# A hybrid streaming encoder step: value parts of forgetting attention whole in a turn's last gap, value transposes ahead of it

## The reference, cut to what matters

```
for l in range(DEPTH):                       # 2 layers, 1024 prompt tokens and 64 sample tokens
    h = rms_norm(xp, ln_mix[l])
    qa, ka, va, la, qb, kb, vb = project_heads(h, w_in[l], b_f[l])
    ...
    # group A, forgetting attention: 8 heads x 64, causal, decay from the cumulative log-forget bias
    s = einsum('bqhd,bkhd->bhqk', q, k) * FOX_SCALE
    p = softmax(where(causal, s + decay, NEG))
    o = einsum('bhqk,bkhd->bqhd', p, v)
    ...
    xp = xp + o @ w_out[l]                   # with group B, sliding-window attention
    xp = xp + cross_attend(rms_norm(xp, ln_mem[l]), w_mq[l], mk, mv, w_mo[l])   # 4 heads x 128, 256 memory tokens
    f, cst = conv_ffn(rms_norm(xp, ln_ffn[l]), ...)
    xp = xp + f
```

## Time and profile before

| what | value |
|---|---|
| median of three timed runs | 3396.98 us (3394.63 to 3397.58) |
| profiled execution, its own time | 3382.89 us |
| its span in the trace | 3381.1 us |
| mean granted clock of TensorE | 0.992 |
| TensorE busy (matmul) | 3227.5 us |
| DVE, ACT, POOL busy | 1897.2, 846.9, 1213.6 us |

### The profile page before, as it was taken

How to read it: one execution, slowest core, us unless ns; L and a number is a source line. 1 busy time by engine, 2 the same in 40 slices (tenths; PEclk the granted TensorE clock), 3 DMA queues, 4 the chain that set the end, 5 groups by cost and what they waited for, 6 DMA issues and landing times.

```text
span 3381.1 us, 50293 instructions
## 1 busy us (share of the span) xinstructions
PE 3227.5 (95%) x20496; PEld 3110.0 (92%) x20496; DVE 1897.2 (56%) x3536; ACT 846.9 (25%) x1960; POOL 1213.6 (36%) x976
## 2 busy tenths in 40 slices
PE   7999998999999999999999999989999999999997
PEld 7888898888899999999988988978889999999997
DVE  6555567676744444444665655577666444444446
ACT  4432323543310000000233333155433000000002
POOL 5213222532434333333442222333424333334331
PEclk9999999999999999999999999999999999999998
DMA  4111222211111111111121112221101111111111
GB/s 160 51 52 45 64 58 69 67 43 33 35 44 47 44 44 44 41 45 46 42 78 58 50 40 58 76 73 48 54 26 41 44 44 46 43 44 47 44 44 65
DMA packets 86021, 177.57 MB, mean 53 GB/s; under 512 B 10544, under 2 KB 13872, under 8 KB 85392
## 3 DMA queue, kind: packets, MB, share of 16 engines
q1 hardware_dynamic: 71968, 132.90, 13.6%
q10 hardware_dynamic: 13824, 41.46, 4.2%
HBM read 150.36 MB, written 16.29 MB: 49 GB/s over the span
## 4 chain that ended last, share of the span: by engine, by line
PE 80%; DVE 11%; ACT 5%; issue 2%; POOL 1%; DMA 0%; ACTq 0%; SPq 0%; DVEq 0%; POOLq 0%
PE PS L614 80%; DVE ACC L1631 2%; ACT PR L1259 1%; DVE HL L1623 1%; DVE PR L1712 1%; DVE XT L1755 1%; ACT PW L1259 1%; DVE PW L1712 1%; ACT PTH L1111 1%; DVE XT L1585 1%; DVE PTL L1557 1%; POOL WL L594 1%; POOL WH L592 0%; DVE DG L1670 0%; ACT G0H L1111 0%
## 5 line engine op out<-in xcount | busy, mean ns | idle before, releaser
L592 POOL TENSOR_TENSOR WH<-RAW,zero 128x512 fp32r<-128x512 f32 x484 | 549.4, 1135 | 2082.0 <-PE PS L614 2067.4
L614 PE MATMUL PS<-HH,WH 128*128 128x384 f32 (+1 forms) x3312 | 863.8, 333 | 41.1 <-DVE HL L1623 16.2
L614 PE MATMUL PS<-HH,WL 128*128 128x384 f32 (+1 forms) x3312 | 848.6, 328 | 0.0
L614 PE MATMUL PS<-HL,WH 128*128 128x384 f32 (+1 forms) x3312 | 848.1, 328 | 0.0
L594 POOL TENSOR_TENSOR WL<-RAW,WH 128x512 fp32r<-128x512 f32 x484 | 669.3, 1383 | 37.9
L614 PEld LDWEIGHTS PS<-HH,WH 128*128 128x128 f32 x3312 | 586.7, 188 | 59.3 <-issue 18.4
L614 PEld LDWEIGHTS PS<-HL,WH 128*128 128x128 f32 x3312 | 589.7, 188 | 0.0
L614 PEld LDWEIGHTS PS<-HH,WL 128*128 128x128 f32 x3312 | 589.0, 188 | 0.0
L1755 DVE TENSOR_TENSOR XT<-PS,XT 128x320 f32<-128x320 f32 x464 | 314.3, 719 | 264.1 <-PE PS L614 263.9
L614 PE MATMUL PS<-G0H,WH 128*128 128x384 f32 (+1 forms) x960 | 274.5, 338 | 25.7 <-DVE XT L1585 17.1
L1111 ACT ACTIVATE PTH<-PS 128x512 fp32r<-128x512 f32 (+4 forms) x320 | 165.9, 521 | 520.1 <-PE PS L614 518.7
(11 more groups left out here) (255 smaller groups left out, 4709.1 us busy)
## 6 DMA issues: line engine op xcount, KB each, us to landing
RAW<-in_slabs SPq DMA_DIRECT2D x484, 256.0 KB, 2.6
XR<-decays ACTq DMA_DIRECT2D x16, 512.0 KB, 5.8
XT<-in_xT SPq DMA_DIRECT2D x8, 544.0 KB, 8.5
out_fk<-T ACTq DMA_DIRECT2D x8, 544.0 KB, 2.7
XR<-decays ACTq DMA_DIRECT2D x16, 272.0 KB, 7.0
out_fv<-T ACTq DMA_DIRECT2D x8, 544.0 KB, 2.9
out_y<-YT ACTq DMA_DIRECT2D x8, 544.0 KB, 3.1
RX<-ST ACTq DMA_DIRECT2D x24, 136.0 KB, 2.5
```

Of the source, the lines that this page charges most:

```text
L592: pool.tensor_tensor(WH[:, s, :], RAW[:, s, :], zero[:, 0:1].to_broadcast([128, HALF]), ALU.add).then_inc(w_hi, 1)
L614: ins = pe.matmul(*a, **k)
```

## The change

Three tables and the places that call for value transposes are edited. In fox_fill the parts of the next pair are dealt two to a turn, in gaps 0 and 1 of the turns 12, 13 and 14, and each value part stands whole in gap 2 of the turns -1, 0 and 1. The value transposes of pairs 1 to 3 are cut in two: the first two groups run in turn 1 behind the scores and ahead of gap 2, the other two in turn 2 behind the scores. V_GROUPS goes from 3, 2, 2, 2 tiles to 3, 3, 2, 1. In mem_fill the first part of head 2's queries stands in the gaps 0 and 1 of turn -1, ahead of the first scores, and the other two in gap 2 of the turns 0 and 1. ACT and DVE call their halves in the same turns.

```diff
@@ fox_fill
-            fill = {n - 1: spread(k[:2], (0, 1, 2)), n: spread(k[2:] + q[2:] + q[:1], (0, 1, 2)), n + 1: spread(q[1:2], (0, 1, 2))}
+            fill = {n - 1: spread(k[:2], (0, 1)), n: spread(k[2:] + q[2:], (0, 1)), n + 1: spread(q[:2], (0, 1))}
             if pair:
                 v = tile_parts(("v", pair), "T32")
-                fill |= {-1: spread(v[:1], (2,)), 0: spread(v[1:2], (0, 1, 2)), 1: spread(v[2:], (0, 1, 2))}
+                fill |= {c - 1: spread(v[c:c + 1], (2,)) for c in range(len(CH))}
@@ mem_fill
-            fill = {c - 1: spread(third[c:c + 1], (0, 1, 2)) for c in range(len(CH))}
+            fill = {c - 1: spread(third[c:c + 1], (2,) if c else (0, 1)) for c in range(len(CH))}
...
-        V_GROUPS = [[0, 1, 2], [3, 4], [5, 6], [7, 8]]
+        V_GROUPS = [[0, 1, 2], [3, 4, 5], [6, 7], [8]]
@@ TensorE
-            def value_hook(pe, filled):
-                value_tiles(pe, T32, V_GROUPS, own_values, filled)
-
+            def value_hook(pe, groups):
+
+
+                value_tiles(pe, T32, groups, own_values, (third_free, place.at("third", 1)))
                 held_groups[:] = [place.at("group", 2)] * len(held_groups)
@@ attention
                         scores(pe, steps[s + 1])
+                    if s in ahead_of_gap:
+                        ahead_of_gap[s]()
                     parts(pe, fill, s, 2)
@@ layer
-                        hooks = {2: lambda: value_hook(pe, (third_free, place.at("third", 1)))}
-                    attention(pe, fox_steps(pair), fox_fill(pair), hooks)
+                        between = {1: lambda: value_hook(pe, V_GROUPS[:2]), 2: lambda: value_hook(pe, V_GROUPS[2:])}
+                    attention(pe, fox_steps(pair), fox_fill(pair), {}, between)
@@ ACT, and DVE likewise
-                    hooks = {2: own_values} if pair else {0: own_values}
+                    hooks = {0: lambda: own_values(V_GROUPS)}
+                    if pair:
+                        hooks = {1: lambda: own_values(V_GROUPS[:2]), 2: lambda: own_values(V_GROUPS[2:])}
```

More of the change, by code:

```diff
@@ L992, in values, with attention @@
                     signal(w_used)
-            def attention(pe, steps, fill, hooks):
+            def attention(pe, steps, fill, hooks, ahead_of_gap={}):
                 rings = [0]
@@ L1026, in layer @@
                 project(pe, ("q", 0), HH, HL, CH)
-                own = project(pe, ("v", 0), HH, HL, CH)
+                project(pe, ("v", 0), HH, HL, CH)
                 pe.wait_ge(const_ok, 5)
@@ L1030, in layer @@
                     if pair == 0:
-                        hooks = {0: lambda: value_hook(pe, own)}
+                        between = {0: lambda: value_hook(pe, V_GROUPS)}
                         if l == 0:
-                            hooks[1] = lambda: mem_stat(pe)
+                            between[1] = lambda: mem_stat(pe)
                     else:
-                        hooks = {2: lambda: value_hook(pe, (third_free, place.at("third", 1)))}
-                    attention(pe, fox_steps(pair), fox_fill(pair), hooks)
+                        between = {1: lambda: value_hook(pe, V_GROUPS[:2]), 2: lambda: value_hook(pe, V_GROUPS[2:])}
+                    attention(pe, fox_steps(pair), fox_fill(pair), {}, between)
                     if pair == 1:
@@ L1355, in layer, with own_values @@
                 for pair in range(PAIRS):
-                    def own_values():
-                        value_groups(act, V_GROUPS, own_rows)
+                    def own_values(groups):
+                        value_groups(act, groups, own_rows)
                     def value_store():
@@ L1848, in own_rows, with own_values @@
                     return 128 if tile < NB else DEC
-                def own_values():
-                    value_groups(dve, V_GROUPS, own_rows)
+                def own_values(groups):
+                    value_groups(dve, groups, own_rows)
                 keys()
```

## The result

| | before | after |
|---|---|---|
| median (lowest to highest), us | 3395.81 (3384.43 to 3397.58), 4 runs | 3356.87 (3356.51 to 3363.65), 4 runs |
| profiled execution, us | 3382.89 | 3357.14 |
| its span, us, and mean granted clock | 3381.1, 0.992 | 3355.3, 0.991 |

The changed kernel is faster: the ratio is 0.9896, interval 0.9865 to 0.9926. I had said 3372 with a range of 3363 to 3384; 3356.87 lies under the range. The two profiled executions differ by 25.8 us, which is near the sum that I had worked out (24.9). The two medians differ by 38.9. So one question of this study was where the other 13 us are.

The account below looks back on a forecast made before the run. TensorE, busy 95% of the span, was taken as the bound, so only its waits could be won. Terms of 9.7, 0.6, 5.9, 0.8, 3.4, 0.7, 3.2 and 0.6 sum to 24.9; 3396.98 - 25 = 3372 us, range 3363 to 3384.

Parts of the forecast that it names:

- Cover: Between value parts and between query parts: other TensorE work hides the evictions, removing 12 waits of 0.81 and 8 of 0.74.
- The split: Value transposes of pairs 1 to 3 in two turns: 3.28 against 3.84 us, 0.56 saved a pair, 3.4 in all.
- The 1.72: Turn 2 of pairs 1 to 3: step 1's transposes come 1.72 us after the scores, a sum of chain pieces.
- The worry about what is queued behind it: Turn 1's new wait and step 0's transposes behind part 2: chains under 2.5 us, beneath 3.5 us of part 2.
- Pair 0: First value transposes of each layer: the wait for V shrinks by 0.35 us a layer, 0.7 in all.
- Memory: Head 2's memory queries: 4 waits of 0.81 go, 3.2 us, plus 0.6 for restarts; the 0.77 diagonal wait stays.
- the carry to the median: Last step: the profiled execution's 14 us below the timed median is kept, so 25 comes off 3396.98, giving 3372.
- A: Whole kernel: the saving comes as summed, 25 us, range 3366 to 3378; chance 0.74.
- B: Value groups and evictions: waits move to new places, only 15 us remain, 3382; chance 0.10.
- C: Stretches at half clock after pair 0's wait: up to 5 and 3 us more come back, 3364; chance 0.08.
- D: Window attention's start: the freed time is waited for later, nothing measurable, 3393 to 3399; chance 0.04.
- E: Value groups 0 and 1 late on ACT shift turn 2: slower by 0.2%, 3404; chance 0.04.

Follow-up runs that it names:

- e3: The kernel before with only the value parts put whole in the last gap, value transposes left in turn 2; 3377.63 us, ratio 0.9966.
- e2: The kernel before with only the next pair's parts dealt two by two; 3383.44 us, ratio 0.9995.
- e4: The kernel before with only the parts of head 2's memory queries moved; 3384.18 us, ratio 0.9998.
- e5: The changed kernel run again without edit, beside the kernel before; 3358.82 us, ratio 0.9903.
- e10: The changed kernel run once more without edit, on another chip beside the kernel before; 3363.27 us, ratio 0.9932.
- e6: The changed kernel with all value transposes of pairs 1 to 3 back in turn 2, groups 3, 2, 2, 2; 3369.65 us, ratio 0.9938 to before.
- e7: The changed kernel with pair 0's value transposes cut in two, over turns 0 and 1; 3358.47 us, ratio 0.9902 to the kernel before.
- e1: The kernel before, unchanged, run again beside itself; 3385.63 us, ratio 0.9999.

## Why the prediction was right, and where it failed

**The working was right, and the sum nearly.** 24.9 us were forecast, 25.8 lie between the two profiles, 27.1 at equal clock. The rows can be added without the fit: 2.65 for each of six pairs, 0.89 for each of eight pair ends and 1.44 for memory in each layer (both below, layer 1 taken as layer 0) are 25.9. So the last 1.2 us of the 27.1 stand in no row that I read.

| part | forecast | at equal clock |
|---|---|---|
| value parts whole (12 waits of 0.81, restarts) | 9.7 + 1.2 for the parts alone | 12.0 (e3) |
| next pair's parts two by two | 5.9 + 0.8 | 8.1 (e2) |
| memory queries | 3.2 + 0.6 | 3.3 (e4) |
| value transposes split, groups, pair 0 | 3.4 + 0.7 - 0.6 for one start more | 4.7 (e5, e10 less e6) |

The parts add to 28.1, the whole is 27.1. The difference is within the fit's error, so no hindrance between them is seen.

*Cover.* All 16 + 8 waits went, as said. The terms for them are a little small (12.0 and 8.1 for 10.9 and 6.7), about 0.1 us for each wait, which is at or just above what the fit can tell. At pair 0's end the trace gives 0.89 us for the 0.84 forecast, or 7.1 for all eight: from query part 2 to pair 1's scores 143.03 to 158.00 after the change, 143.43 to 159.29 before.

*The split.* I had called this the least sure term. It follows from 176.99 to 184.83, 7.84 us, where before took 9.95: 2.11 less, to set against the 1.56 us that six tiles cost in turn 1, which turned out as 1.31 (172.09 to 173.40). That is 0.80 a pair and 4.8 in all, beside the 4.7 of e6 and the 3.4 forecast: this is the term that was sized too small, since twelve transposes cost less in turn 1 than the 0.122 us each that I had taken from before. The 1.72 that I had built up from four rows was measured as 1.73. The worry about what is queued behind it did not come true: step 0's transposes wait 0.60 for PTL, as before.

*Pair 0.* 0.7 us forecast, and in the waits it is nothing: 2.09 and 2.36 became 1.85 and 2.70. In layer 0 my reason held, two matmuls more lie ahead of the same release. In layer 1 the chain itself began late. DVE's rows there, after the change:

```profile
1728.68 1.28 DVE L1717 CUSTOM_DVE_ANT_0 PR<-PS,XR,big 128x1024 f32<-128x1024 f32 x1 [0.81 <-DMA XR<-decays]
...
1733.48 1.02 DVE L1562 TENSOR_TENSOR V<-PS,V 128x384 fp32r<-128x384 f32 x2 [3.08 <-ACT V L1114]
```

The same maxima waited 0.25 us for that load before. Here time freed earlier was waited for again, 0.56 us of it.

*Memory.* From the start of the first part to step 1's transposes it is 16.20 us (745.70 to 761.90) after, 17.64 before (758.85 to 776.49): 1.44 less in layer 0 for the 1.9 forecast. No wait is left behind the shortest cover, six matmuls that take 0.82 us from start to the next part (755.17 to 755.99). I had said that the wait of 0.77 for the diagonal stays as it is; it grew, and is 0.97 in e4, e5 and e10 too:

```profile
761.90 1.16 PE L614 MATMUL PS<-DG,PW 128*128 128x128 f32 x8 [0.98 <-DVE DG L1675]
```

**The step that failed** is the last one, the carry to the median: "The difference is carried to the median: 3396.98 - 25". I took the 14 us between the profiled execution and the median of three for something that belongs to every timed run. It belongs to the clock of single executions. The kernel before runs at any level from 0.984 to 0.993, its times from 3381.6 to 3406.8 go with it, and of 69 later runs only a quarter came out at 3395 or more; its median over them is 3387.70. The changed kernel's first four runs stood at 0.990 to 0.992. So of the 38.9 us between the medians shown, some 27 are the change, and some 12 are that three of the four runs of before took far longer than its usual time, while those of after were near their shortest. The clocks of the first three runs of before are not listed; that they stood near 0.987, as runs of 3396.9 do, is inferred from the table and not seen. Had the sum been taken from the profiled execution, 3382.89 - 25, it would have given 3358, and 16 runs of the changed kernel have a median of 3358.8. Nor was the measured time outside the range by luck alone: 3358.8 lies under it too. The range was drawn from what the change might do, and held no room for the spread of one kernel's executions.

**The rivals.** A was right in its mechanism, and its own range (3366 to 3378) suffers from the same step. B, the waits move, was wrong for this change, though right for e7. C spoke of the clock, but of two stretches in the changed kernel. Those did change somewhat: 77.5 to 87.4 went from 0.52 to 0.66, and e10's execution has 0.83 there. In all, windows of 5 us give seven stretches at half clock before and eight after. I had called a change of that number a sign of being wrong, but it is none: e1, with no change at all, has thirteen. The mean clock over all runs is 0.9895 before and 0.9902 after, 1.8 us by the slope. What C should have asked is at which clock the *before* was timed. D and E did not occur.

## What to carry to other kernels

Here every wait of TensorE behind the eviction of its own bank went entirely once other work of at least that length stood between (0.81 us from start to start, printed as 0.65). Sum such waits from the distances of starts, not from what is printed, and add what a saved restart costs, here 0.1. If the profiled execution and the median of a few runs differ by more than the runs should, find out by the granted clock which of them is unusual before adding anything: a forecast made from a trace belongs to that trace's clock. To tell 3 to 8 us in 3,400, compare at equal granted clock, since medians of 12 runs could not, and look at the clock itself beside it, since an edit could change that too.

## What the runs showed of the hardware that I had not expected

The kernel runs on one core, TensorE is busy for 95%, and still executions of the same program differ by 0.7% (3381.57 to 3406.81 us), in a nearly continuous row of clock levels. Each 0.001 of mean clock is worth 2.65 us. The stretches at 1.2 GHz are the end of the span, where TensorE is mostly idle in both executions, and short ones elsewhere. Each of the six short ones in the kernel before has a wait of 1.63 to 3.58 us in it or just ahead of it; but e1 has one from 2225 to 2235, and from 2200 to there no wait of TensorE is longer than 0.97. Waits of 0.20 to 0.66 inside dense work left the granted clock at 1.00 (after the change, 140 to 187):

```profile
140.00:187.00 47.00, 45.53 (x303) 42.72 (x302) 21.11 (x50) 11.37 (x25) 19.52 (x17) 1.00 0.26 76
```

e1's mean clock of 0.987 against 0.992 over some 3,390 us means about 34 us more at half clock (0.005 x 2 x 3,390); it took 13.8 us longer. The Trainium skill, TensorE: Matmul & The Clock Gate, section Terms, prices such time at half its length, which would be 17 us by an estimate. These two executions give less, four fifths of it, and so does the fit (2.65 us for 0.001, where half of 6.8 us is 3.4). The row pair of e1 above shows one reason: some of the time lost was a wait before.
